# State-space chunk loop: decay groups formed two ahead, clamp moved to ScalarE, and the skip, gate and mean square taken into the loop

## The reference, cut to what matters

```python
L = jnp.exp(segsum(A))                                  # decays inside a chunk
CB = jnp.einsum('bclgn,bcsgn->bgcls', Cc, Bc)
y_diag = jnp.einsum('bgcls,bgjcls,bcsgjp->bclgjp', CB, L, X)
...
y = y_diag + y_off                                      # y_off: from the state at the chunk's start
y = y + d_skip[:, None] * xs
y = rms_norm(y * jax.nn.silu(z), norm_w)                # mean square over 1024 channels
out = jnp.concatenate([y, o_gla]) @ w_out
```

## Time and profile before

| quantity | value |
|---|---|
| profiled execution | 2053.71 us |
| its span, first to last instruction | 2051.6 us |
| median of three executions | 2057.56 us |
| mean granted TensorE clock | 0.91 of full speed |
| busy share of the span | PE 92%, PEld 83%, DVE 51%, ACT 34%, POOL 17% |
| `ssd_chunks` | 1357.0 to 1477.4 us of the span |
| last block of `ssd` | 1478.7 to 1498.3 us |

### The profile page before, as it was taken

How to read it: one execution, slowest core, us unless ns; L and a number is a source line. 1 busy time by engine, 2 the same in 40 slices (tenths; PEclk the granted TensorE clock), 3 DMA queues, 4 the chain that set the end, 5 groups by cost and what they waited for, 6 DMA issues and landing times. The chain is left out here.

```text
span 2051.6 us, 31526 instructions
## 1 busy us (share of the span) xinstructions
PE 1888.7 (92%) x12982; PEld 1713.1 (83%) x12982; DVE 1043.1 (51%) x1828; ACT 689.4 (34%) x1355; POOL 352.4 (17%) x514
## 2 busy tenths in 40 slices
PE   8997998898999999989998969788779999999997
PEld 8995555598999999988798958545479899999997
DVE  6563553257666663237462134336564766666224
ACT  4642442235333332225263221111132533333213
POOL 0110230032222220110100010123103222221110
PEclk9995798799999999999899978568699899999998
DMA  5201720021322222231121230100132222222221
GB/s 189 73 23 59 222 83 22 4 90 52 93 83 83 83 80 76 84 105 51 60 73 64 84 123 1 47 0 1 82 98 69 70 83 83 83 83 82 84 85 62
DMA packets 52049, 152.40 MB, mean 74 GB/s; under 512 B 7091, under 2 KB 18803, under 8 KB 51267
## 3 DMA queue, kind: packets, MB, share of 16 engines
q1 hardware_dynamic: 51906, 150.40, 23.0%
HBM read 138.12 MB, written 16.39 MB: 75 GB/s over the span
## 5 line engine op out<-in xcount | busy, mean ns | idle before, releaser
L767 PE MATMUL ps<-x_high,w_high 128*128 128x288 f32 x2288 | 693.0, 303 | 26.3 <-DVE x_low L1435 15.0
L768 PE MATMUL ps<-x_low,w_high 128*128 128x288 f32 x2288 | 683.6, 299 | 0.0
L769 PE MATMUL ps<-x_high,w_low 128*128 128x288 f32 x2288 | 681.5, 298 | 0.0
L767 PEld LDWEIGHTS ps<-x_high,w_high 128*128 128x128 f32 x2288 | 437.7, 191 | 36.5 <-DVE x_low L1435 21.7
L769 PEld LDWEIGHTS ps<-x_high,w_low 128*128 128x128 f32 x2288 | 439.3, 192 | 0.0
L768 PEld LDWEIGHTS ps<-x_low,w_high 128*128 128x128 f32 x2288 | 438.4, 192 | 0.3
L744 DVE TENSOR_TENSOR w_low<-w_raw_ahead,w_high 128x1024 fp32r<-128x1024 f32 (+1 forms) x128 | 154.3, 1207 | 231.7 <-ACT w_high L739 231.5
L739 ACT ACTIVATE w_high<-w_raw_ahead 128x1024 fp32r<-128x1024 f32 (+1 forms) x128 | 130.8, 1024 | 272.5 <-PE ps L769 245.2
L767 PE MATMUL ps<-g_high,w_high 128*128 128x288 f32 x704 | 209.0, 297 | 1.7 <-ACT ub L876 1.7
L768 PE MATMUL ps<-g_low,w_high 128*128 128x288 f32 x704 | 210.0, 298 | 0.0
L769 PE MATMUL ps<-g_high,w_low 128*128 128x288 f32 x704 | 209.2, 297 | 0.0
(11 more groups left out here) (423 smaller groups left out, 2690.1 us busy)
## 6 DMA issues: line engine op xcount, KB each, us to landing
w_raw_ahead<-in_w_up SPq DMA_DIRECT2D x44, 512.0 KB, 3.5
w_raw<-in_w_up SPq DMA_DIRECT2D x44, 512.0 KB, 3.6
w_raw_ahead<-in_w_odd SPq DMA_DIRECT2D x36, 512.0 KB, 3.2
w_raw<-in_w_even SPq DMA_DIRECT2D x19, 512.0 KB, 3.4
w_raw_ahead<-in_w_down SPq DMA_DIRECT2D x16, 512.0 KB, 3.5
w_raw<-in_w_down SPq DMA_DIRECT2D x16, 512.0 KB, 3.5
ptok<-in_cache_tok SPq DMA_DIRECT2D x32, 192.0 KB, 2.5
w_raw_ahead<-in_w_mix SPq DMA_DIRECT2D x16, 384.0 KB, 3.2
```

Source lines behind the costliest of these rows:

```text
L767: pe.matmul(out, self.high[:, s, at, :], high(k)[:, cols], start=(k == 0), stop=False)
L768: pe.matmul(out, self.high[:, s, at, :], low(k)[:, cols], start=False, stop=False)
L769: return pe.matmul(out, self.low[:, s, at, :], high(k)[:, cols], start=False, stop=(k == kt - 1))
```

## The change

- `sum_decays` runs two slots ahead instead of one.
- The clamp becomes `gap` on ScalarE: relu(own decay − other decay), four instructions a slot, and the exponential takes it with a scale of −1. ScalarE's order is gap(s + 1), then the exponential of slot s.
- VectorE's mask product runs one slot ahead: iteration s holds mask(s + 1). VectorE also adds the skip term (`add_skip`), ten instructions of up to 128x512.
- GpSimd multiplies x with d (`skip`, ten instructions) and y with silu(z) (`gate`, nine; the tenth is on VectorE). ScalarE squares each half tile in the loop (`square`, ten) at odd slots from 5 on; each waits for GpSimd's gate.
- The mean square: after the last slot TensorE runs `rms` for five token tiles, eight products each, with the squares as weights and one column of 1/1024 as the moving operand, so that it lands with tokens on partitions; five small copies, a root and a reciprocal of a 128x5 tile, and six products with the identity spread it over PSUM banks 6 and 7. L1564 reads it from there.
- `load_ahead` moves to the beginning of the chunk block. The end of the block waits for `spread` and for the stores. The last block of `ssd` goes.

```diff
@@ TensorE
                 sum_decays(0)
+                sum_decays(1)
...
-                    if s + 1 < SLOTS:
-                        sum_decays(s + 1)
+                    if s + 2 < SLOTS:
+                        sum_decays(s + 2)
...
+                def rms(n):
+                    cols, m = tok(TILE[n])
+                    pe.wait_ge(squared, 2 * n + 2)
...
+                    for j in range(8):
+                        mm = pe.matmul(net.ps[0:m, XS, n:n + 1], zt[:, j, cols], net.inv_d, start=(j == 0), stop=(j == 7), ...)
+                for n in range(TT):
+                    rms(n)
+                pe.wait_ge(rstd_done, 1)
+                pe.wait_ge(kv_used, n_kv)
...
+                            mm = pe.matmul(net.ps[:, 6 + lo // HT, ...], rstd[0:m, n:n + 1].broadcast_to([m, P]), net.ident[...], ...)
+                mm.then_inc(spread, 1)
@@ ScalarE
+                def gap(s):
+                    act.wait_ge(decays, s + 1)
+                    if s >= 3:
+                        act.wait_ge(y_done, s - 2)
+                    for i in range(4):
+                        ins = act.activation(L[0:m, s % 3, i, 0:m], net.ps[0:m, D[s % 2], P * i:P * i + m], ACT.Relu, scale=-1.0, bias=per[...])
+                    ins.then_inc(clamped, 1)
...
+                    if s + 1 < SLOTS:
+                        gap(s + 1)
                     act.wait_ge(clamped, s + 1)
-                    act.activation(L[...], L[...], ACT.Exp).then_inc(exped, 1)
+                    act.activation(L[...], L[...], ACT.Exp, scale=-1.0).then_inc(exped, 1)
...
+                    if s % 2 and s >= 5:
+                        square((s - 5) // 2)
@@ GpSimd
+                    if q % 2 == 0:
+                        skip(s // 2)
+                        if s >= 4:
+                            gate(s // 2 - 2)
+                gate(2 * TT - 2)
@@ VectorE
-                        clamp(s + 1)
-                    dve.wait_ge(exped, s + 1)
...
+                        mask(s + 1)
...
+                    if s and q % 2 == 0:
+                        add_skip(s // 2 - 1)
                 sum_y(TT - 1, 1)
+                add_skip(2 * TT - 1)
+                dve.tensor_tensor(y, y, zt[:, 4:8, cols], ALU.mult).then_inc(gated, 1)
                 add_states(SLOTS - 1)
+                ... (five copies to rstd, reciprocal)
@@ SyncE
+                net.load_ahead(sp, io["w_mix1"], 6)
                 sp.wait_ge(kv_used, n_kv)
                 net.store(sp, io["ssd_s_p"], hs_p[:])
                 net.store(sp, io["ssd_s_s"], hs_s[:])
+                sp.wait_ge(spread, 1)
+                net.all_stored(sp)
```

More of the change, by code:

```diff
@@ L2361, in _, with ssd_chunks @@
                 net.store(sp, io["gla_s_s"], ss[:])
-def ssd_chunks(net, c, xbc, cum, per, DL, hs_p, hs_s, cat):
+def ssd_chunks(net, c, small, zt, xbc, cum, per, DL, hs_p, hs_s, cat):
     nc, io = net.nc, net.io
@@ L2386, in ssd_chunks @@
         L = sb("L", [P, 3, 4, P])
+        stat = net.stat[:].rearrange("p a i j -> p (a i j)")
+        rstd = stat[:, 0:TT]
+        gated, squared, rms_done, varied, rooted, rstd_done, spread = (net.sem(n) for n in (
+            "gated", "squared", "rms_done", "varied", "rooted", "rstd_done", "spread"))
+        skipped, added, initialised = net.sem("skipped"), net.sem("added"), net.sem("initialised")
         (zeroed, order, decays, clamped, exped, mixed, y_done, y_summed, off_done, xs_turned, xdt_done, xdd_done, bcb_done,
@@ L2488, in keep_b, with square @@
                     act.activation(bt[0:m, n % 2, :, :], split_free(net.ps[0:m, BCB, 0:256], g=2, n=P), ACT.Copy).then_inc(b_kept, 1)
+                def gap(s):
+                    n, q = divmod(s, 4)
+                    _, m = tok(TILE[n])
+                    act.wait_ge(decays, s + 1)
+                    if s >= 3:
+                        act.wait_ge(y_done, s - 2)
+                    for i in range(4):
+                        ins = act.activation(L[0:m, s % 3, i, 0:m], net.ps[0:m, D[s % 2], P * i:P * i + m], ACT.Relu, scale=-1.0,
+                                             bias=per[0:m, TILE[n], 0, 4 * q + i:4 * q + i + 1])
+                    ins.then_inc(clamped, 1)
+                def square(v):
+                    n, g = divmod(v, 2)
+                    cols, _ = tok(TILE[n])
+                    z = zt[:, 4 * g:4 * g + 4, cols]
+                    act.wait_ge(gated, v + 1)
+                    act.activation(z, cat[:, 4 * g:4 * g + 4, cols], ACT.Square).then_inc(squared, 1)
+                gap(0)
                 keep_b(0)
@@ L2493, in _ @@
                     _, m = tok(TILE[n])
+                    if s + 1 < SLOTS:
+                        gap(s + 1)
                     act.wait_ge(clamped, s + 1)
[L2495 removed]
+                    act.activation(L[0:m, s % 3, :, 0:m], L[0:m, s % 3, :, 0:m], ACT.Exp, scale=-1.0).then_inc(exped, 1)
                     if q == 2 and n + 1 < TT:
                         keep_b(n + 1)
+                    if s % 2 and s >= 5:
+                        square((s - 5) // 2)
+                square(2 * TT - 2)
+                square(2 * TT - 1)
+                act.wait_ge(varied, 1)
+                act.activation(rstd, rstd, ACT.Sqrt, bias=net.eps).then_inc(rooted, 1)
             @block.gpsimd
@@ L2513, in decay, with skip, gate @@
                     return pool.tensor_tensor(hs, hs, DL[:, s:s + heads, at:at + 1].broadcast_to([P, heads, 64]), ALU.mult)
+                def skip(v):
+                    n, g = divmod(v, 2)
+                    cols, m = tok(TILE[n])
+                    x = xbc[:, 4 * g:4 * g + 4, cols]
+                    pool.wait_ge(xs_turned, v + 1)
+                    pool.tensor_tensor(x, x, small[:, 2 + 4 * g:6 + 4 * g, None].broadcast_to([P, 4, m]), ALU.mult).then_inc(skipped, 1)
+                def gate(v):
+                    n, g = divmod(v, 2)
+                    cols, m = tok(TILE[n])
+                    y = cat[:, 4 * g:4 * g + 4, cols]
+                    pool.wait_ge(added, v + 1)
+                    pool.tensor_tensor(y, y, zt[:, 4 * g:4 * g + 4, cols], ALU.mult).then_inc(gated, 1)
                 leave(0, 0)
@@ L2536, in _ @@
                 link = Chain(dve, order)
[L2538 to L2548, removed]
                 def scale_xs(n, g):
@@ L2574, in sum_y, with mask, add_skip @@
                     dve.tensor_tensor(out, y, out, ALU.add).then_inc(y_summed, 1)
+                def mask(s):
+                    n, q = divmod(s, 4)
+                    _, m = tok(TILE[n])
+                    l = L[0:m, s % 3, :, 0:m]
+                    dve.wait_ge(exped, s + 1)
+                    dve.wait_ge(cb_kept, n + 1)
+                    dve.tensor_tensor(l, l, cbm[0:m, n % 2, q // 2:q // 2 + 1, 0:m].broadcast_to([m, 4, m]), ALU.mult).then_inc(mixed, 1)
+                def add_skip(v):
+                    n, g = divmod(v, 2)
+                    cols, m = tok(TILE[n])
+                    y = cat[:, 4 * g:4 * g + 4, cols]
+                    dve.wait_ge(y_summed, v + 1)
+                    dve.wait_ge(skipped, v + 1)
+                    dve.tensor_tensor(y, y, xbc[:, 4 * g:4 * g + 4, cols], ALU.add).then_inc(added, 1)
                 def add_states(s):
@@ L2587, in _ @@
                 dve.memset(hs_p[:], 0.0).then_inc(zeroed, 1)
-                clamp(0)
+                dve.memset(stat, 1.0).then_inc(initialised, 1)
                 scale_xs(0, 0)
                 mask_cb(0)
+                mask(0)
                 scale_xs(0, 1)
@@ L2609, in _ @@
                             scale_xs(n + 1, q // 2)
+                    if s and q % 2 == 0:
+                        add_skip(s // 2 - 1)
                 sum_y(TT - 1, 1)
-                add_states(SLOTS - 1)
+                add_skip(2 * TT - 1)
+                cols, m = tok(TILE[TT - 1])
+                y = cat[:, 4:8, cols]
+                dve.wait_ge(added, 2 * TT)
+                dve.wait_ge(gated, 2 * TT - 1)
+                dve.tensor_tensor(y, y, zt[:, 4:8, cols], ALU.mult).then_inc(gated, 1)
+                add_states(SLOTS - 1)
+                dve.wait_ge(initialised, 1)
+                dve.wait_ge(rms_done, TT)
+                for n in range(TT):
+                    _, m = tok(TILE[n])
+                    ins = dve.tensor_copy(rstd[0:m, n:n + 1], net.ps[0:m, XS, n:n + 1])
+                ins.then_inc(varied, 1)
+                dve.wait_ge(rooted, 1)
+                dve.reciprocal(rstd, rstd).then_inc(rstd_done, 1)
             @block.sync
             def _(sp):
+                net.load_ahead(sp, io["w_mix1"], 6)
                 sp.wait_ge(kv_used, n_kv)
@@ L2684, in _ @@
                 dve.tensor_copy(EA[:, :, TP:T], split_free(net.bank(0), j=8, n=NS))
[L2686 to L2722, removed]
+        ssd_chunks(net, c, small, zt, xbc, cum, per, DL, hs_p, hs_s, cat)
 def even_mixer(net, cat):
```

15 lines of the change are left out of this document (11 added, 4 removed).

## The result

Four executions of the changed kernel took 2017.19 to 2027.7 us, median 2024.62; the kernel before 2048.86 to 2078.17, median 2065.52. The ratio of the changed to the former is 0.987, 95% interval 0.985 to 0.990; it goes by the runs counted as fast, so it is not the quotient of the two medians, which is 0.980. The profiled execution took 2017.19 us, span 2015.4.

What follows compares the result with a forecast made beforehand. TensorE was taken as the bound, waiting on each slot's chain of decays, clamp, mask and product and partly at the low clock. Five terms sum to −32.3 us from the profiled 2053.71: 2021, range 2011 to 2042.

Steps and rivals of the forecast that it cites:

- Terms 1 and 2: Head of the chunk loop, −2.0 us (0 to −3.7), and its first full tile, −4.3 us (−3 to −8).
- Term 5: Tail behind the last y product, 25.7 us, through stores or mean square: 20.4 us, −5.3 (−8.3 to +1.4).
- Term 3: Two middle tiles of 23.82 us become 18.6 each: −10.4 us together (−7 to −12.8).
- The charge of 1.2 a tile: Added to 17.4 us of TensorE work per tile for squares waiting on GpSimd's gates and for clashes.
- Term 4: Last tile to its last y: 21.75 us becomes 11.4, stalls of 1.5 included, −10.3; −4.0 at the low clock.
- I take it to hold once up: TensorE's clock in the new, mixed loop: claimed to stay high once reached, as in the GLA loop at 1.00.
- The second rival: GpSimd and VectorE block one another on their shared port: 20.5 us a tile, −24 us, 2030; chance 0.16.
- The first and third rival: First: clock behaves as before, only idle time goes, 2038.6 us, chance 0.24. Third: low clock through whole loop, 2076.6, 0.08.
- At nothing: L1564 with its PSUM operand, charged at no time because TensorE works on products ahead of it.
- The gap: ScalarE's four gap instructions a slot: 1.2 to 2.5 us, taken as 1.5, covered with 1 to 3 us to spare.

Runs made afterwards that it cites:

- early_stores: Changed kernel with the large store of the small states cut into eight batches, each stored after its last addition: ratio 0.983 to the kernel before.
- loop_only: Kernel before with only decay sums two groups ahead, clamp on ScalarE and mask one ahead, old pointwise block kept: ratio 0.978 to the kernel before.
- moved_late: Changed kernel with the skip's product on ScalarE, its addition on GpSimd, and squares two groups later: ratio 0.985 to the kernel before.
- late_squares: Changed kernel with every square two groups later on ScalarE, nothing else changed: ratio 0.981 to the kernel before.
- early_both: Changed kernel with the large store in eight pieces and column sums of tiles 0 to 2 in the last tile's loop: ratio 0.981 to the kernel before.
- moved_add: Changed kernel with the skip's product on ScalarE and its addition on GpSimd ahead of the gate: ratio 0.984 to the kernel before.
- no_gate: Changed kernel without GpSimd's nine gates, squares waiting for VectorE's additions instead: ratio 0.979 to the kernel before.
- no_add: Changed kernel without the skip's multiplications and additions, gates and squares kept: ratio 0.981 to the kernel before.

## Why the prediction was right, and where it was not

The time, 2024.62, is 3.6 us from the forecast of 2021, and its direction came from the mechanism named. But the block gave 27.6 of the 32.3 us forecast, and the unchanged stages ahead of it helped by 7.5 in this profile. The ratio of 0.987 likewise comes to about 26 us. That the median came so near the forecast is therefore partly luck.

- **Terms 1 and 2** depend on where the head is cut. By the prediction's own cut, at the transposes, the head gave 1.2 us of 2.0 and the first full tile 3.7 of 4.3; cut at the y products of slot 4 they gave 2.05 and 2.8. Either way they gave about 4.9 of 6.3 together.
- **Term 5** holds: the tail gave 5.6 (forecast 5.3). Both paths of the tail end within 2 us of each other: SP waits 13.4 us for the store and then 1.6 for the spread, as early_stores confirms. The products took 13.8 us, within the 10 to 16 given.
- **Term 3** came out at 10.0 of 10.4. Its bare work of 17.4 a tile is 17.0 and 16.4 in loop_only. The charge of 1.2 a tile for the moved work was too small: 2.5 and 1.9.
- **Term 4** is the mis-sized one, 7.2 of 10.3. The last tile ran at 0.65 and took 14.6 us; the sentence that failed is "I take it to hold once up". In tiles 2 and 3 it holds where there are no waits, as loop_only and moved_late show. In the last tile it fell in every profile here, in those two as well, without a wait and for 3.4 us. Their last tile of 11.45 us meets the 11.4 of the term by luck: the 1.5 us charged for stalls did not come, and the low clock cost about as much.
- **The second rival** is at work inside the forecast, and so are two signs listed as wrong: squares that wait for gates with gaps behind them, and masks of over 1.2 us (up to 1.73 in tiles 2 and 3). By the Trainium skill's page "SBUF — State Buffer", section "SBUF: two separate sides", the loser of the shared port stands still for the other's whole instruction; the 1.75 us addition beside a 1.71 gate agrees in kind. moved_late shows what the rival left out: GpSimd may do as much, and draw the masks out as much (128x512 masks took 1.03 us on average there, 1.07 in the changed kernel, 0.85 in loop_only), without a wait of TensorE, once VectorE has no additions beside them and ScalarE's gaps stand behind no waiting square.
- **The first and third rival** are out for tiles 2 and 3, which ran at 0.91 and 1.00; the last tile, at 0.65, lies between the first rival and the forecast.
- **At nothing** fits for L1564 with its PSUM operand: behind the block the kernel took 550.8 us instead of 552.0.
- **The gap** took 1.14 us for four instructions, below the 1.2 given as its lower end; the four clamps took 1.13. The rule of the Trainium skill's page "ScalarE: Activation LUTs", section "Rules for kernel authors", that relu belongs on VectorE decided nothing here.

What stays open: what starts a low stretch and how long it lasts. Many began during a wait of TensorE or within 2 us behind it, but not all waits had one: 0.66 us at slot 14 of the changed kernel and 0.35 at slot 10 of late_squares were followed by none. The wait of 0.67 at slot 10 was followed by 3.4 us at the low clock in both profiles of the changed kernel, and by 27 in early_stores, early_both and moved_add. In the last tile the clock fell without a wait in loop_only, no_gate and moved_late (3.4 us each) and in no_add (13.6).

## What to carry to other kernels

An operation that waits for a slower engine must not stand in a queue ahead of one that feeds the bound: put it later, where what it waits for has long been done. Price moved work where it lands, and test each half of a change alone; here the half that fills the bound engine gave all, and the other half took back more than its own stage won until its order was mended. And look at the clock behind each wait of TensorE: waits of under 1 us were often, though not always, followed by low clock that cost more than they did.

## What had not been expected of the hardware

- The same 499 instructions kept TensorE busy for 84.8 to 119.1 us, at granted clocks of 0.82 and 0.58. A profile of the same kernel differs too: 89.9 and 93.9 us. The Trainium skill's page "TensorE: Matmul & The Clock Gate", section "Part 1: The HAM clock gate", has it that the number of products at the low clock differs between runs of one kernel; the two profiles agree.
- A gate of 1.27 us on GpSimd and a VectorE addition of 0.69 that meet are both drawn out, to 1.71 and 1.75 (late_squares, 1418.69). The mask ahead of the addition, drawn out to 1.34 itself, still ran when the gate began.
